# Feed-forward groups on 512-column prompt tiles, with the samples' tokens as stationary operand

## What is computed

```python
x = x + 0.5 * gt1 * swiglu(modulate(x, norm_ffn1, sh1, sc1), ffn1_w_gu, ffn1_w_down)
m = parallel_heads(modulate(x, norm_mix, sh2, sc2), ...)      # RWKV-7 heads and attention heads
x = x + gt2 * m
x = x + 0.5 * gt3 * swiglu(modulate(x, norm_ffn2, sh3, sc3), ffn2_w_gu, ffn2_w_down)
# swiglu(h, w_gu, w_down): gate, up = split(h @ w_gu); (silu(gate) * up) @ w_down
```

## Time and profile before

| | |
|---|---|
| runs | 2474.67, 2476.42, 2476.98 us; median 2476.42 us |
| profiled execution, its own time | 2474.27 us |
| span of its trace, first to last instruction | 2472.2 us |
| TensorE busy (PE) | 2378.3 us, 96% |
| weight loads (PEld) | 2259.0 us, 91% |
| VectorE busy (DVE) | 1107.2 us, 45% |
| ScalarE busy (ACT) | 387.5 us, 16% |
| GpSimd busy (POOL) | 537.4 us, 22% |
| mean granted TensorE clock | 0.982 |

### The profile page before, as it was taken

One profiled execution on the slowest core, in us unless ns is written; L12 is line 12 of the kernel. 1 busy time (PEld: TensorE's weight loads), 2 busy tenths in 40 slices (PEclk: granted clock), 3 DMA queues, 4 the chain that ended last, 5 costly groups with the idle time before them and its releaser, 6 DMA issues. The chain is left out here.

```text
span 2472.2 us, 50589 instructions
## 1 busy us (share of the span) xinstructions
PE 2378.3 (96%) x21666; PEld 2259.0 (91%) x21666; DVE 1107.2 (45%) x2446; ACT 387.5 (16%) x890; POOL 537.4 (22%) x278
## 2 busy tenths in 40 slices
PE   5999999999999999999888899999999999999997
PEld 4999999999999989888568885999999999999997
DVE  4524443334444364434576664147333444433344
ACT  4100000000000132434521123140000000000003
POOL 3312121212112032111331134313211212122111
PEclk8999999999999999999899998999999999999999
DMA  9232221111011142100310002332111011111101
GB/s 336 86 103 87 83 85 52 47 38 50 18 51 51 38 116 63 35 27 24 112 57 5 4 12 63 107 103 68 52 34 51 17 51 51 51 51 34 51 9 73
DMA packets 160620, 151.22 MB, mean 61 GB/s; under 512 B 21474, under 2 KB 141971, under 8 KB 160074
## 3 DMA queue, kind: packets, MB, share of 16 engines
q1 hardware_dynamic: 159946, 146.75, 19.0%
q10 hardware_dynamic: 144, 2.23, 0.2%
q0 software_dynamic: 384, 0.07, 0.0%
HBM read 137.98 MB, written 11.34 MB: 60 GB/s over the span
## 5 line engine op out<-in xcount | busy, mean ns | idle before, releaser
L476 PE MATMUL bank<-hh,f_up_hi 128*128 128x364 f32 (+1 forms) x2112 | 696.2, 330 | 11.6 <-ACT hh L416 9.4
L478 PE MATMUL bank<-hh,f_up_lo 128*128 128x364 f32 (+1 forms) x2112 | 694.3, 329 | 0.0
L477 PE MATMUL bank<-hl,f_up_hi 128*128 128x364 f32 (+1 forms) x2112 | 694.3, 329 | 0.0
L1189 DVE TENSOR_TENSOR f_prod<-f_silu,bank 128x364 f32<-128x364 f32 x132 | 70.2, 532 | 777.2 <-PE bank L478 777.2
L476 PEld LDWEIGHTS bank<-hh,f_up_hi 128*128 128x128 f32 x2112 | 397.4, 188 | 17.7 <-issue 17.1
L477 PEld LDWEIGHTS bank<-hl,f_up_hi 128*128 128x128 f32 x2112 | 397.4, 188 | 0.0
L478 PEld LDWEIGHTS bank<-hh,f_up_lo 128*128 128x128 f32 x2112 | 397.4, 188 | 0.0
L491 DVE SCALAR_TENSOR_TENSOR x<-bank,mods,x 128x364 f32<-128x364 f32 (+1 forms) x544 | 306.1, 572 | 202.5 <-PE bank L478 187.0
L944 POOL TENSOR_TENSOR f_up_lo<-f_up_raw,f_up_hi 128x2048 fp32r<-128x2048 f32 x44 | 203.1, 4616 | 787.0 <-DVE f_up_hi L1176 787.0
L476 PE MATMUL bank<-f_a_hi,f_dn_hi 128*128 128x364 f32 (+1 forms) x1056 | 348.2, 330 | 0.8 <-DVE f_scratch L494 0.8
L478 PE MATMUL bank<-f_a_hi,f_dn_lo 128*128 128x364 f32 (+1 forms) x1056 | 346.9, 328 | 0.0
(11 more groups left out here) (377 smaller groups left out, 2806.1 us busy)
## 6 DMA issues: line engine op xcount, KB each, us to landing
f_up_raw<-in_ffn_w_gu SPq DMA_DIRECT2D x88, 512.0 KB, 5.0
f_dn_raw<-in_ffn_w_down SPq DMA_DIRECT2D x22, 1024.0 KB, 7.6
ada<-in_w_ada SPq DMA_DIRECT2D x12, 1024.0 KB, 16.3
late<-in_w_ada SPq DMA_DIRECT2D x12, 1024.0 KB, 5.0
w_in_raw<-in_w_in SPq DMA_DIRECT2D x16, 512.0 KB
gates<-in_w_ada SPq DMA_DIRECT2D x8, 1024.0 KB, 7.1
x_in<-in_x_prompt SPq DMA_DIRECT2D x8, 512.0 KB, 8.2
gate<-in_w_ada SPq DMA_DIRECT2D x4, 1024.0 KB, 5.1
```

The costliest lines, as they stand in the source:

```text
L476: pe.matmul(out, wh, rh, start=(n == 0), stop=False)
L477: pe.matmul(out, wh, rl, start=False, stop=False)
L478: ins = pe.matmul(out, wl, rh, start=False, stop=(n == last))
L1189: dve.tensor_tensor(prod[u % 2][:, 0:n], silu[u % 2][:, 0:n], k.psum[2 * (u % 2) + 1][:, 0:n], ALU.mult).then_inc(up_free, 1)
```

## The change

Groups 1 to 9 of both feed-forward parts get a new form; groups 0 and 10 keep the three tiles.

- The prompt is cut into two tiles of 512 columns (`PTILES`), without the samples. A group has 4 units `u` of 48 matmuls, and 16 units `v` of 6 matmuls; the `v` use three banks (4, 5, 6) in turn.
- The samples' 64 tokens are laid side by side as high and low part (`h_s`, 128 columns per chunk) and become the stationary operand. The group's weights of both chunks, gate and up half, move past them: 16 matmuls of 512 columns into bank 7 (`sample_up`, ahead of unit 3). Rows 0 to 63 of the result are the high part's, rows 64 to 127 the low part's.
- ACT copies bank 7 to SBUF (`sample_copy`). Behind unit 3, four fp32 matmuls of 64 columns against a folded identity turn it feature-major and add the two halves (`sample_turn`, bank 6). ACT takes silu, DVE multiplies and splits (`sample_swish`, `sample_gated`).
- The down-projection of the samples is row-major: `a_s` is stationary, the down weights move, 4 matmuls of 512 columns for each half of the output (`sample_down`, behind v = 7 and v = 11). DVE adds the bank to `acc` (`sample_sum`).
- In group 10, behind its first unit, eight fp32 matmuls of 64 columns fold `acc` to feature-major (`fold_samples`), and DVE applies the gates of the sequences and adds to `x` (`samples_folded`).
- `gated` works in place in the `silu` buffer. `up_head(0)` moves behind unit 3 and `sample_gated`, `up_head(1)` behind the sum of v = 12. SP loads the down weights ahead of the second chunk's up weights.
- In the modulation groups the products stand behind unit 0, behind unit 1, behind the gate half of unit 2 and behind its up half, and use bank 5.
- `acc` and `h_s` lie where the second part of the constants lay; these are now loaded in group 10 of `f1`. The folded identity moves to the first part.

The core of the diff:

```diff
+PTILES = [(0, 512), (512, 512)]
+            def sample_up(g):
+                pe.wait_ge(dn_free, sums_of(g) + 4)
+                pe.wait_ge(s_added, 2 * g - 1)
+                for c in range(KD):
+                    for part in range(2):
+                        ins = pe.matmul(bank_s[:].rearrange("p (j n) -> p j n", j=FC), k.h_s[:, c],
+                                        up_split[:, :, part, c].rearrange("p j h n -> p j (h n)"),
+                                        start=(c == 0 and part == 0), stop=(c == KD - 1 and part == 1))
+                ins.then_inc(s_up, 1)
+            def sample_turn(g):
+                pe.wait_ge(s_copied, g)
+                for i in range(2 * FC):
+                    ins = pe.matmul(bank_f[:, NS_TOK * i:NS_TOK * i + NS_TOK], s_rows[:, P * i:P * i + P], k.c("ident_folded"),
+                                    start=True, stop=True)
+                ins.then_inc(s_turned, 1)
+            def prompt_down(g, t, c):
+                a, n = PTILES[t]
+                if c == 0:
+                    pe.wait_ge(act_done, units_of(g) + NPT * (FC - 1) + t + 1)
+                v = KD * t + c
+                if v == 2:
+                    pe.wait_ge(s_act, g)
+                pe.wait_ge(dn_free, sums_of(g) + max(v + 2, 4))
+                three_passes(pe, k.psum[4 + v % 3][:, 0:n], ...
+            def sample_down(g, h):
+                if h == 1:
+                    pe.wait_ge(s_added, 2 * g)
+                for f in range(FC):
+                    for w in (dn_hi, dn_lo):
+                        ins = pe.matmul(bank_s[:], a_s[:, f], w[:, f, D // 2 * h:D // 2 * h + D // 2],
+                                        start=(f == 0 and w is dn_hi), stop=(f == FC - 1 and w is dn_lo))
+                ins.then_inc(s_dn, 1)
             def group(g, modulation=False):
...
+                for u in range(MU):
+                    if u % NPT == 0:
+                        pe.wait_ge(up_lo_done, FC * g + u // NPT + 1)
+                    if u == MU - 1:
+                        sample_up(g)
+                    for h in range(2):
+                        prompt_up(g, u, h)
+                        if modulation and (u, h) in LATE_AT:
+                            q = LATE_AT.index((u, h))
+                            if q == 0:
+                                pe.wait_ge(dn_free, sums_of(g) + 4)
+                            late.product(pe, q, 0, 4 * g + q - 3)
+                sample_turn(g)
                 if modulation:
                     late.turn(pe, g - 1, late_turned)
-                downs(g)
+                pe.wait_ge(dn_lo_done, g + 1)
+                for t in range(NPT):
+                    for c in range(KD):
+                        prompt_down(g, t, c)
+                        if (t, c) in ((0, KD - 1), (1, 3)):
+                            sample_down(g, t)
...
             def group(g, modulation=False):          # DVE
...
+                for u in range(MU):
+                    gated(g, u, u // NPT, *PTILES[u % NPT])
+                    if modulation and u == MU - 2:
                         late.copy(dve, g)
+                sample_gated(g)
+                up_head(0, FC * g + FC + 1, units_of(g) + MU)
                 if modulation:
                     late.add(dve, g - 1, g + 2, late_turned)
+                for v in range(MD):
+                    prompt_summed(g, v)
+                    if v in (KD - 1, KD + 3):
+                        sample_sum(g, v // KD)
+                    if v == KD + 4:
+                        up_head(1, FC * g + FC + 2, units_of(g) + MU)
+                dn_head(g + 2, sums_of(g) + MD)
```

More of the change, by code:

```diff
@@ L212, in __init__ @@
         self.qkv = self.at("qkv", QKV_AT, [P, 6, T])
+        self.acc = self.at("sample_sums", up32(CONST_AT + 4 * sum(CONST_COL["spread"])), [P, D])
+        self.h_s = self.at("h_s", up32(CONST_AT + 4 * sum(CONST_COL["spread"])) + 4 * KB, [P, KD, 2 * NS_TOK], F32R)
     def at(self, name, off, shape, dt=F32):
@@ L1024, in downs, with prompt_up @@
                         down(g, t, c)
-            def group(g, modulation=False):
[L1027 to L1036, removed]
+            def prompt_up(g, u, h):
+                j, (a, n) = u // NPT, PTILES[u % NPT]
+                free, done = ((gate_free, gate_mm), (up_free, up_mm))[h]
+                pe.wait_ge(free, units_of(g) + u + 1)
+                three_passes(pe, k.psum[2 * (u % 2) + h][:, 0:n],
+                             [(up_hi[j][:, c, h, :], up_lo[j][:, c, h, :], k.hh[:, c, a:a + n],
+                               k.hl[:, c, a:a + n]) for c in range(KD)]).then_inc(done, 1)
@@ L1037, in group, with fold_samples @@
                 if modulation:
                     late.turn(pe, g - 1, late_turned)
-                downs(g)
+                pe.wait_ge(dn_lo_done, g + 1)
[4 more added lines that the diff above has]
+                            sample_down(g, t)
                 if modulation:
                     pe.wait_ge(late.added, g)
+            def fold_samples():
+                pe.wait_ge(dn_free, sums_of(NGRP - 1) + 4)
+                pe.wait_ge(s_added, 2 * (NGRP - 1) - 1)
+                for c in range(KD):
+                    ins = pe.matmul(k.psum[4][:, NS_TOK * c:NS_TOK * c + NS_TOK], k.acc[:, P * c:P * c + P], k.c("ident_folded"),
+                                    start=True, stop=True)
+                ins.then_inc(acc_turned, 1)
@@ L1151, in _, with sample_copy, sample_swish @@
                 norm.highs(act, 2, False)
-            for u in range(NU):
[L1153 to L1156, removed]
+            def sample_copy(g):
+                act.wait_ge(s_up, g)
+                act.copy(s_rows[:], bank_s[:]).then_inc(s_copied, 1)
+            def sample_swish(g):
+                act.wait_ge(s_turned, g)
+                act.activation(scratch[:], s_turned_cols[:, :, 0], ACT.Silu).then_inc(s_silu, 1)
+            for u in range(NU):
+                swish(0, u, TILES[u % NT][1])
+            with act.Fori(1, NGRP - 1) as g:
+                for u in range(MU):
+                    if u == MU - 1:
+                        sample_copy(g)
+                    swish(g, u, PTILES[u % NPT][1])
+                sample_swish(g)
+            for u in range(NU):
+                swish(NGRP - 1, u, TILES[u % NT][1])
             if first:
@@ L1197, in summed, with sample_sum, prompt_summed @@
+            def sample_sum(g, h):
+                dve.wait_ge(s_dn, 2 * g - 1 + h)
+                acc = k.acc[:, D // 2 * h:D // 2 * h + D // 2]
+                dve.tensor_tensor(acc, acc, bank_s[:], ALU.add).then_inc(s_added, 1)
             def summed(g, v, banks=4):
                 t, c = v // KD, v % KD
[L1199 removed]
+                dve.wait_ge(dn_mm, sums_of(g) + v + 1)
                 add_gated(dve, k, i_gate, c, t, k.psum[4 + v % banks], scratch[:, v % 2]).then_inc(dn_free, 1)
[L1202 to L1208 removed]
+            def prompt_summed(g, v):
+                c, (a, n) = v % KD, PTILES[v // KD]
+                dve.wait_ge(dn_mm, sums_of(g) + v + 1)
+                dve.scalar_tensor_tensor(k.x[:, c, a:a + n], k.psum[4 + v % 3][:, 0:n], k.mod(i_gate, c), k.x[:, c, a:a + n],
+                                         ALU.mult, ALU.add).then_inc(dn_free, 1)
@@ L1237, in first_group @@
             def first_group():
+                dve.memset(k.acc[:], 0.0).then_inc(s_added, 1)
+                dve.drain()
+                dve.tensor_copy(k.h_s[:, :, 0:NS_TOK], k.hh[:, :, now])
+                dve.tensor_copy(k.h_s[:, :, NS_TOK:], k.hl[:, :, now]).then_inc(hs_done, 1)
                 for u in range(NU):
-                    gated(0, u)
+                    gated(0, u, u // NT, *TILES[u % NT])
                     if u == 0:
```

134 lines of the change are left out of this document (83 added, 51 removed).

## The result

The changed kernel takes 2489.27 us (median of 6 runs, 2484.37 to 2494.04), beside 2475.39 us for the kernel before in the same comparison (6 runs, 2474.25 to 2476.98): the ratio is 1.0056, with an interval of 1.0041 to 1.0072. It is slower by 13.9 us where I had forecast 2444.8 us and a gain. The profiled execution took 2486.08 us with a span of 2484.1, 11.9 above the span before.

A forecast was written before the change was run, and what follows sets the result against it. TensorE, busy 96% of the span, was taken to bound the kernel: plain groups -39.8, modulation groups +6.0 and fold +2.2 make -31.6 us, so 2476.42 becomes 2444.8 us, range 2416 to 2492.

The forecast's parts named there:

- The price of one matmul: Plain group on TensorE: a 512-column matmul costs 220.0 ns at 2.4 GHz, so 312 take 68.64 us.
- the stream is paid in blocks: Reading behind the 220.0 ns: matmul columns are paid in blocks of 32, with 6.7 ns left over.
- rival C: Fixed 14.8 ns on every matmul whatever its length; 228.1 ns at 512 columns, 2487.6 us, slower; chance 0.22.
- The turn: Behind unit 3, four fp32 matmuls for the samples: 0.6 us a group, bounds 0.4 and 0.8.
- The wait at v = 3: TensorE waits for bank 4, freed by DVE's sum of v = 0: 0.4 us a group, bounds 0 and 1.5.
- Rival E: Matmul costs 220 ns, but the three-bank ring and turn lose 1.5 us more a group: 2472 us; chance 0.09.
- Rival "doesn't do what it says": Two-piece moving weights might stream slower: 16 of 312 matmuls, doubled 3.5 us a group, +63; no chance of its own.
- Modulation groups: Three groups: product loads make TensorE wait 1.6 us, then 0.2 us twice; 2.0 us each, +6.0 us together.
- No cost: Moved `up_head(1)` at v = 12, `dn_head` and POOL's 4.6 us are all in time: nothing added.
- The fold: Eight small fp32 matmuls at some 0.12 us and the change of type: 1.1 us, twice, +2.2 us.
- Group 0: DVE's clearing of `acc` and copies of `h_s`, about 2 us before its first multiplication, come in time for TensorE.
- The constants' move: Second constants leave the start, where TensorE's long wait is for ACT: nothing, bounds -2 and 0 us.

The follow-up runs named there:

- e5: Kernel before, looped groups' up-projection runs of 24 matmuls reading twelve other stretches of the normalised input, 352 to 512 columns; output not the reference's; 2517.59 us.
- e6: Kernel before, looped groups' up-projection runs of 24 matmuls reading twelve further stretches, 256 to 512 columns; output not the reference's; 2531.18 us.
- e4: Changed kernel with the four fp32 matmuls of the samples' turn issued twice; 2506.62 us.
- e7: Changed kernel with `up_head(1)` behind the sum of v = 10 instead of v = 12; 2483.99 us, beside 2471.48 for the kernel before.
- e1: Kernel before, groups 1 to 9: down-projection matmuls reading 256 to 512 columns, third tile with 64 or 32 weight columns; output not the reference's; 2475.36 us.
- e2: Kernel before with tiles of 368, 368 and 352 columns in place of 364, 364 and 360, projections too; 2456.59 us, ratio 0.9932.

## Why the prediction was wrong

- **The price of one matmul, "I take 220.0": this is the step that failed.** It rested on the reading "the stream is paid in blocks". Measured: 226.7 ns, and e5 and e6 show no blocks. The 6.67 ns on 312 matmuls are 2.08 us a group and 37.4 us over 18 groups, more than the whole forecast gain of 31.6 us. The law of rival C holds in the main: a surplus of about one size, 13.3 ns rather than the 14.8 I gave it, rides on 256 and on 512 columns alike. "It decides once a 512-column matmul costs more than 226 ns" was borne out: at 226.7 the plain group is even, and what comes on top makes the kernel slower. That 2489.3 us lies so near C's 2487.6 is in part luck: C's plain group was 0.2 us too long, 4 us over 18, and its +7 for modulation and fold was 13.2. The evidence that misled me, 360 and 364 columns at one price, was real; but the few cycles by stretch are as large as the 1.7 ns that the difference in length is worth. I took an exact law from a difference of that size. That the place of the 360 columns made up for their length is argued; (728, 360) wasn't read by itself.
- By the Trainium skill (TensorE: Matmul & The Clock Gate, section "Back-to-back issue gap") 512 columns would cost 215.8 ns and 256 would cost 109.2, estimates by its formula for isolated matmuls, which I took for the stream; for a stream with weight loads the same section states about 131 ns at 512. The runs show 226.7 and 119.9, so they contradict both.
- **The turn, 0.6 us: 0.90.** It lay above my upper bound. I counted instructions; each of these fp32 matmuls runs as two records. The two instructions of the earlier trace rows, from which I took the price, are transposes (`pe.transpose`), and they left one record each. The turn's 0.3 us more on 18 groups are 5.4 us.
- **The wait at v = 3, 0.4 us: about 0.1.** TensorE's rows there:

```profile
641.88 0.39 PE L485 MATMUL bank<-f_a_hi,f_dn_lo 128*128 128x512 f32 x1
642.11 0.44 PE L483 MATMUL bank<-f_a_hi,f_dn_hi 128*128 128x512 f32 x1
642.39 0.40 PE L484 MATMUL bank<-f_a_lo,f_dn_hi 128*128 128x512 f32 x1
```

  The step behind the first matmul of v = 3 is 0.28 where 0.23 is the rule. In e4, where TensorE comes 0.8 us later, the step is 0.23: so it was the wait. TensorE came there later than I counted, because the turn and every matmul were dearer. Rival E is refuted. The plain group adds up: 312 x 0.2267 = 70.7, the 16 `sample_up` matmuls at 233 ns add 0.1, turn 0.9, wait 0.1: 71.8.
- **Rival "doesn't do what it says"**: the two-piece moving operand costs 233 ns in place of 226.7, 0.1 us a group where I had bounded it by 3.5.
- **Modulation groups, +6.0 us over the plain group's change: +9.7.** The mechanism was right and the wait for the first product was forecast at 1.6 us; it was 1.8, 2.5 and 2.5, 6.7 in sum, with 1.6 us of lower clock once; the other 1.3 us aren't traced. The part I missed is DVE's rounding beside POOL, 1.8 us in each of the second and the third group: I moved `up_head(1)` later and costed that at nothing ("No cost"), counting only its load and its deadline. What it collides with sits on the way to SP's load. e7 shows that, and that without it those two waits would have been 0.6 and 0.7, less than I forecast. The third and fourth product didn't wait. My 0.2 us each was a slip: by my own terms the load lands 6.27 us after the start of the product before it and TensorE is back after 6.5, which is cover and not a wait.
- **The fold, 1.1 us twice: 1.8 and 1.7.** The same error as with the turn; 16 records for 8 matmuls:

```profile
813.32 1.89 PE L1132 MATMUL bank<-const,sample_sums 128*128 128x64 f32 x16
```

- **Group 0, "TensorE needs that multiplication's bank only in the second half of unit 2": +1.0 us in the second part.** The bank was in time, the weights weren't. TensorE's timeline there:

```profile
1690.82 0.38 PE L290 MATMUL bank<-const,mod_rows 128*128 128x128 f32 x2
1691.79 0.44 PE L483 MATMUL bank<-hh,f_up_split 128*128 128x364 f32 x1 [0.58 <-POOL f_up_split L969]
```

  POOL's:

```profile
1687.13 4.60 POOL L969 TENSOR_TENSOR f_up_split<-f_up_raw,f_up_split 128x2048 fp32r<-128x2048 f32 x1 [7.22 <-DVE f_up_split L1285]
```

  DVE's:

```profile
1685.84 1.22 DVE L1285 CAST f_up_split<-f_up_raw 128x2048 fp32r<-128x2048 f32 x1
```

  DVE's clearing and copies delay the rounding of the second up weights, POOL's subtraction stands behind it and TensorE behind that. The first matmul starts 0.97 us behind the turn, where it was 0.13 before (1681.44 to 1681.57 us), so this is 0.84 of the 1.0 us. In the first part no matmul waited for these weights. There the group's +0.7 is the lower clock of the start, which lasted 4.3 us into the group and 2.8 before; e4 and e7, with the same code there, took 77.3 us as the kernel before did (77.2).
- **The constants' move, nothing:** +1.0 us at the start, within the scatter of the other profiles (54.8 to 56.6 us).

## What to carry to other kernels

When fewer but longer instructions are meant to save their fixed part, measure that fixed part at both lengths before anything is built on it: a few units reading other stretches of the same buffer are enough. Two lengths that are 1% apart tell little about a law when the price has a scatter of 1% by itself. When a step is moved on one engine, look at what it will run beside on its new place, and read the price of an fp32 matmul from rows of the same kind of instruction, counting its records.

## What the runs showed of the hardware

- An fp32r matmul of n columns costs n/2.4 GHz + about 13.3 ns (28 to 48 cycles, mostly 28 to 37) in a stream with changing weights, from 256 to 512 columns, and n/1.2 GHz with nothing besides at the lower clock level: 427 ns for 512. What the 32 cycles are stays open. 256 and 512 columns pay the same (e5, e6), and 64 or 32 columns of weights in place of 128 save at most 5 of them (e1).
- Where a tile of one length starts is worth up to 3.4 ns a matmul (368 columns: 165.5 at 352, 168.9 at 368), and tiles of 368, 368 and 352 in place of 364, 364 and 360 columns gained 0.7% (e2).
- A DVE cast of 0.35 us can take 4.35 us beside a POOL subtraction. DVE's timeline in the changed kernel, 0.46 us behind the start of POOL's instruction at 1687.13:

```profile
1687.59 4.35 DVE L1300 CAST f_a_hi<-f_silu 128x364 fp32r<-128x364 f32 x1
1692.01 0.54 DVE L1302 TENSOR_TENSOR f_a_lo<-f_silu,f_a_hi 128x364 fp32r<-128x364 f32 x1
```

  The trace of the kernel before has it too, 0.45 us behind the start of POOL's subtraction at 1675.98, so the collision could have been read there before anything was moved:

```profile
1676.43 4.36 DVE L1192 CAST f_a_hi<-f_prod 128x364 fp32r<-128x364 f32 x1
```

- A wait of 2.5 us on TensorE was followed by the lower clock in one group of the changed kernel and not in the next; in e4 waits of 2.44 and 2.47 us were both followed by it.
